# Four per-token tensors of a delta-rule recurrence, turned by quarter-array products with the identity instead of full-array transposes

## The reference, cut to what matters

```
def step(state, inp):
    r_t, w_t, k_t, v_t, a_t, b_t = inp
    sa = jnp.einsum('bhvk,bhk->bhv', state, a_t)
    state = (state * w_t[:, :, None, :] + sa[..., None] * b_t[:, :, None, :]
             + v_t[..., None] * k_t[:, :, None, :])
    return state, jnp.einsum('bhvk,bhk->bhv', state, r_t)
```

## Time and profile before

| | |
|---|---|
| median of 3 runs | 1745.68 us (1744.81 to 1747.44) |
| the profiled execution | 1743.47 us |
| its span | 1741.7 us |
| TensorE busy (matmul) | 1667.7 us, 96% of the span |
| VectorE, ScalarE, GpSimd busy | 771.3, 561.9, 451.8 us |
| instructions | 34694 |
| the recurrence | about 150 to 480 us of the span |

### The profile page before, as it was taken

How to read it: one execution, slowest core, us unless ns; L and a number is a source line. 1 busy time by engine, 2 the same in 40 slices (tenths; PEclk the granted TensorE clock), 3 DMA queues, 4 the chain that set the end, 5 groups by cost and what they waited for, 6 DMA issues and landing times. The chain is left out here.

```text
span 1741.7 us, 34694 instructions
## 1 busy us (share of the span) xinstructions
PE 1667.7 (96%) x15178; PEld 859.4 (49%) x15178; DVE 771.3 (44%) x1061; ACT 561.9 (32%) x883; POOL 451.8 (26%) x236
## 2 busy tenths in 40 slices
PE   5999999998999998899999999999999999999997
PEld 2454666666545555444444445444444444444443
DVE  5696666655325455213111487332332323232328
ACT  5323544554325555311312165421212212121300
POOL 2221322222110012023423022651423233232310
PEclk9999999999999999999999999999999999999999
DMA  9851000000010200412110310430202021112002
GB/s 360 284 179 32 15 23 20 4 28 27 27 50 23 62 1 1 145 37 60 48 37 24 109 49 25 141 101 13 84 24 72 24 72 36 60 36 84 1 1 97
DMA packets 105773, 109.69 MB, mean 63 GB/s; under 512 B 2592, under 2 KB 82610, under 8 KB 105394
## 3 DMA queue, kind: packets, MB, share of 16 engines
q1 hardware_dynamic: 105648, 107.82, 19.3%
HBM read 101.52 MB, written 4.19 MB: 61 GB/s over the span
## 5 line engine op out<-in xcount | busy, mean ns | idle before, releaser
L218 PE MATMUL tokens_ps<-a_hi,z 128*128 128x512 bf16 x896 | 231.1, 379 | 0.0
L674 PE MATMUL ff_ps<-ff_hi,c_hi 128*128 128x512 bf16 x512 | 194.0, 379 | 0.9 <-DVE z L2577 0.9
L674 PE MATMUL ff_ps<-ff_lo,c_hi 128*128 128x512 bf16 x512 | 194.0, 379 | 0.0
L674 PE MATMUL ff_ps<-ff_hi,c_lo 128*128 128x512 bf16 x512 | 194.0, 379 | 0.0
L2577 DVE TENSOR_TENSOR z<-ff_ps,z 128x512 f32<-128x512 f32 x128 | 88.3, 690 | 205.0 <-PE ff_ps L674 204.4
L2473 ACT ACTIVATE ff_r<-tokens_ps,cols 128x1024 f32<-128x1024 f32 x30 | 33.4, 1114 | 421.4 <-PE tokens_ps L218 414.4
L2399 POOL TENSOR_TENSOR z<-z 128x1024 bf16<-128x1024 f32 x28 | 62.5, 2232 | 345.9 <-ACT z L2395 345.9
L218 PEld LDWEIGHTS tokens_ps<-a_hi,z 128*128 128x128 bf16 x896 | 87.6, 98 | 105.8
L2565 DVE TENSOR_TENSOR ff_r<-ff_r 128x1024 f32<-128x1024 f32 x32 | 41.1, 1284 | 219.1 <-ACT ff_r L2473 219.1
L218 PE MATMUL tokens_ps<-a_lo,z 128*128 128x512 bf16 x448 | 133.2, 379 | 0.0
L195 POOL TENSOR_TENSOR mg_wlo<-mg_stage,mg_whi 128x1024 bf16<-128x1024 f32 x21 | 45.7, 2178 | 158.1 <-ACT mg_whi L191 158.1
(11 more groups left out here) (395 smaller groups left out, 3142.8 us busy)
## 6 DMA issues: line engine op xcount, KB each, us to landing
ff_st<-w_ff SPq DMA_DIRECT2D x8, 2048.0 KB, 7.7
z<-w_ff SPq DMA_DIRECT2D x30, 512.0 KB, 4.0
ada_w<-w_ada SPq DMA_DIRECT2D x6, 2048.0 KB, 8.2
z<-w_in SPq DMA_DIRECT2D x18, 512.0 KB, 4.6
z<-w_ada SPq DMA_DIRECT2D x8, 1024.0 KB, 13.5
mg_stage<-w_in SPq DMA_DIRECT2D x16, 512.0 KB, 4.0
zs_stage<-w_in SPq DMA_DIRECT2D x8, 512.0 KB, 7.3
ada_w<-w_ada SPq DMA_DIRECT2D x4, 1024.0 KB, 13.5
```

The source lines that it names most:

```text
L218: last = pe.matmul(out[:, h * HALF:(h + 1) * HALF], w[:, kt, :], a[:, slot, h * HALF:(h + 1) * HALF], start=(x == 0 and y == 0), stop=(x = ...
L674: last = pe.matmul(out, a[:, slot, at], w[:, x, n], start=(x == 0 and y == 0), stop=(x == k - 1 and y == 2))
```

## The change

Each of the four tensors is now made by 16 products of 64x64x64 with the identity: for each of four column blocks, each of two chunks and each of two heads e, one product whose stationary operand is the 64x64 piece of the tensor. Head e goes to bank BA or BB, so every tensor now fills half of both banks, and ScalarE reads it out in two copies of 128x256, one for each bank. Since every tensor uses both banks, the waits move up: `kn` now waits for the copies of `vn`, `bn` for those of `kn`, `an` for those of `bn`, and `mv` for those of `an`.

```diff
-            def natural(t, name, dst, ps):
+            def natural(t, name, dst):
                 wait(act, t, name + "T")
-                act.activation(dst, ps, ACT.Copy).then_inc(s[name + "e"], 1)
+                for e in range(2):
+                    act.activation(dst(e), BAB[e][:, 0:2 * P].rearrange("p (j n) -> p j n", n=HD), ACT.Copy).then_inc(s[name + "e"], 1)
...
-                natural(t, "vn", flat(vn[:]), BA[:])
+                natural(t, "vn", lambda e: vn[:, :, e * HD:(e + 1) * HD])
...
-                natural(t, "bn", W[f][:, :, 1, :].rearrange("p (e j) n -> p j e n", e=2), q4(BA).rearrange("p j (e n) -> p j e n", e=2))
-                natural(t, "an", rhs[:, :, 0:HD].rearrange("p (e j) n -> p j e n", e=2), q4(BB).rearrange("p j (e n) -> p j e n", e=2))
+                natural(t, "bn", lambda e: W[f][:, 4 * e:4 * e + 4, 1, :])
+                natural(t, "an", lambda e: rhs[:, 4 * e:4 * e + 4, 0:HD])
...
-            def natural(t, name, src, ps):
+            def natural(t, name, src):
                 for j in range(NT):
-                    last = pe.transpose(ps[:, j * P:(j + 1) * P], src[:, j * P:(j + 1) * P], ident)
+                    for c2 in range(2):
+                        at = (2 * j + c2) * CH
+                        for e in range(2):
+                            last = pe.matmul(BAB[e][rows2[c2], j * HD:(j + 1) * HD], src[heads[e], at:at + CH], ident[heads[e], heads[e]], start=True, stop=True)
                 last.then_inc(s[name + "T"], 1)
...
                 wait(pe, t, "KhT")
-                natural(t, "kn", kh, BB)
+                wait(pe, t, "vne")
+                natural(t, "kn", kh)
...
-                wait(pe, t, "vne")
-                natural(t, "bn", bh, BA)
+                wait(pe, t, "kne")
+                natural(t, "bn", bh)
...
-                wait(pe, t, "kne")
-                natural(t, "an", ar[f][:, 0, :], BB)
+                wait(pe, t, "bne")
+                natural(t, "an", ar[f][:, 0, :])
...
-                wait(pe, t, "bne")
+                wait(pe, t, "ane")
                 for e, j, b in blocks:
...
-                for name in ("TTm", "T12e", "ane", "mve"):
+                for name in ("TTm", "T12e", "mve"):
                     wait(pe, t, name)
```

More of the change, by code:

```diff
@@ L984, in phase_recurrence @@
         BAB, BCD, HY = (BA, BB), (BC, BD), (HY0, HY1)
-        per_turn = {"nd": 2, "M1e": 2, "NTd": 2, "NTm": 2, "PQa": NT, "M2e": 2, "TTm": 2, "T12e": 2, "ze": 2, "ge": 2, "ysb": 2, "PQ": 2, "TTe": 4, "Te": 5, "X": 4, "Xe": 4, "TX": 4,
+        per_turn = {"vne": 2, "kne": 2, "bne": 2, "ane": 2, "nd": 2, "M1e": 2, "NTd": 2, "NTm": 2, "PQa": NT, "M2e": 2, "TTm": 2, "T12e": 2, "ze": 2, "ge": 2, "ysb": 2, "PQ": 2, "TTe": 4, "Te": 5, "X": 4, "Xe": 4, "TX": 4,
                     "ch": NC, "S": NC}
@@ L1261, in turn @@
                 decays(n)
-                natural(t, "kn", flat(kn[:]), BB[:])
+                natural(t, "kn", lambda e: kn[:, :, e * HD:(e + 1) * HD])
                 dense_high(t + 2)
@@ L1857, in turn @@
                 shifted(pe, 8, t)
-                natural(t, "vn", zs(8, t), BA)
+                natural(t, "vn", zs(8, t))
                 if t == 0:
```

## The result

The changed kernel takes 1746.4 us (median of 12 runs, 1742.61 to 1752.12), the one before, run beside it, 1743.19 us (12 runs); ratio 1.0024 with a 95% interval of 1.0013 to 1.0034. That ratio is 4.2 us slower (2.3 to 5.9); the two medians lie 3.2 us apart. Forecast were 5.8 us. The time itself was forecast as 1751.5 us and came out 5.1 us lower; 2.5 us of that is the kernel before, whose median was 1745.68 us in three runs and is 1743.19 us here.

The account below looks back on a forecast made before the run. The recurrence was taken to go as fast as TensorE gets through its list; -1.4 + 0.6 + 4.8 + 2.0 = +6.0 us on the profiled or median time gave 1751.5 us, range for 8 in 10 1743.5 to 1758.

Parts of the forecast that it names:

- TensorE's own time: Array time of the four tensors' sets and their neighbours: -1.4 us over turns 1 to 7, +0.6 us in turn 0.
- ScalarE and the waits: Two copies for one and waits moved up in the recurrence: 0 us, upper ends +5 us and +4.6 us.
- The instruction stream: TensorE's instruction blocks run out in dense places of the recurrence: +4.8 us in turns 1 to 6, +2.0 in turn 7.
- The seven blocks: 896 more matmul records in the recurrence were to need seven more instruction blocks, 9.0 a turn instead of 8.1.
- the spacing of 127: TensorE's issue gaps in the recurrence were to stand 126 or 127 matmul records apart, at block edges.
- the refill: Time for the next instruction block to reach TensorE: taken as 3.8 us, with 3.6 and 4.0 as ends.
- the +4.8 us of turns 1 to 6: Added waiting for instruction blocks in the recurrence, +0.8 us for each of these turns.
- The walk over all possible edges: Turn 4's list cut into blocks from 21 starting points: 0.9 us of gaps a turn before, 1.7 after.
- the rival: The instruction stream keeps up in the recurrence; only TensorE's own time counts, -0.8 us, 1744.9 us; chance 0.24.

Follow-up runs that it names:

- the waits alone: Kernel before with its transposes in their old banks, each tensor copied out in two parts and all four waits moved up; ratio 1.0004 to the kernel before.
- the doubled products: Changed kernel with each of its identity products made twice in place, 64 records a set instead of 32; ratio 1.0196 to the kernel before.
- the padding: Kernel before with four loads of a 4-column weight that no matmul uses behind each dense matmul; 1749.6 us, ratio 1.0033.

## Why the prediction was right, step by step

**TensorE's own time: right for the sets, hardly seen in the sum.** Predicted 0.12, 0.13, 0.10 and 0.07 us saved for a set of 0.46, 0.09 paid at `squares` and `bonus`. Set and `chain` together went from 0.84 to 0.74 in the second profile of the changed kernel; a set is 0.52 us to the `chain` (326.20 to 326.72 above), not 0.46, but `chain` is then shorter by 0.03. The bonus product went from 0.97 to 1.06 us (333.40 to 334.46). The sum of a turn is 0.21 us instead of 0.24. In the turns as wholes this saving is hardly seen: without their gaps turns 1 to 6 take 225.9 us instead of 226.2, 0.3 less where six times 0.2 was said. In turn 0 the sets take 0.63 instead of 0.49: +0.6 to +0.7, as said, and among the profiles with the clock at 0.95 that turn takes 37.4 us instead of 36.7.

**ScalarE and the waits: right.** No row of TensorE's waits names a copy of the four tensors, and the waits alone leave the time as it was.

**The instruction stream: the mechanism right, its size somewhat high.** The seven blocks, the spacing of 127 and the refill of 3.4 to 3.9 us came as said. The packets of q8 add what the prediction could only infer, that a gap ends with the arrival of a block.

The term was +6.8 us, the gaps "12 to 16 us instead of 7.1". Measured are 10.2 and 8.8, below that range; on average 9.5 instead of 5.5: +4.0, or +5 if one takes the 4.1 us by which the recurrence grew and adds the 0.9 that the array saved. By turns, the average of two profiles against that of four:

| | forecast | recurrence | gaps |
|---|---|---|---|
| turn 0 | +0.6 | +1.2 | 0 |
| turns 1 to 6 | +3.6 (-1.2 + 4.8) | +1.8 | +2.2 |
| turn 7 | +1.8 (-0.2 + 2.0) | +1.1 | +1.8 |
| sum | +6.0 | +4.1 | +4.0 |

So the part that was sized too high is the +4.8 us of turns 1 to 6. It took 0.8 us for each of them; the gaps there grew by 0.36 a turn, and against the two profiles of the kernel before alone by 0.09 (4.7 instead of 4.2 us in six turns). Turn 4, which I had worked through, paid nothing: its gaps sum to 1.1 and 0.7 us in the two profiles of the changed kernel, against 1.2 and 0.9 in those of the kernel before, and where I had worked out one of 0.8 between `vn` and `an`, there is one of 0.25 or 0.4. The walk over all possible edges with its 0.8 a turn rested on two assumptions that no run measures, a fixed refill time and a list read 16 records ahead. The 7.1 us of the one profile that I had was one draw of something that goes from 2.3 to 8.4. And my argument for the rival named turns 0 and 5 as free of gaps; turn 1 was free of them too. That the total came as near as it did, 4.2 or 5.6 us for 5.8, is in part luck: the terms of single turns missed in both directions.

The rule of the Trainium skill ("Runtime: NRT & Kernel Launch", section "Instruction fetch mechanics"), by which the next block is fetched while the present one is executed and the crossing is mostly hidden, holds here for most edges only: where a block is worked off in less than a refill, it fails. 1536 loads that cost the array next to nothing made the kernel 5 us slower. The measurement decides.

**What stays open.** Why the gaps of one and the same list of TensorE vary from 2.3 to 8.4 us; how much of the 4 to 5 us falls to which turn, which needs more profiles than two; why records are missing in some profiles; some 3 us in the doubled products. That fetching is the cause of the gaps rests on their spacing, the block count, the time of the packets and the padding; the moment at which a block is asked for was not varied by itself.

## What to carry to other kernels

Count instructions as well as array time. Where small products follow each other fast, a block of some 127 matmul records with their loads took at least 3.4 us here, whatever they compute, and adding records in a slow place made the fast places wait. To see whether a gap is one of these, look for a packet of the instruction queue some 2.5 us before its end. Before splitting a transpose into quarter products, try it by rows of the array: half the columns, a transpose's single pass, and here one block more instead of seven.

## What the runs showed of the hardware

- Eight transposes of 64x128 in float32, in two row groups into two banks, took 0.39 us; four of 128x128 0.58 us, sixteen products of 64x64x64 0.52, eight products of 64x128x64 1.04.
- A semaphore increment in TensorE's stream cost about 62 ns amid matmuls of 0.216 us (95 us for 1536); a weight load of 4 columns none that shows in the distance of these matmuls.
- The packets of TensorE's instruction blocks, 16 KB each, never started less than 3.2 us apart in the recurrence. A gap ended 2.2 to 3.1 us after the start of a packet (134 of 135), and in 106 of 135 cases the next packet started 0.9 to 1.5 us later.
